# The odd layer's input projection with seven block products per set in place of eight

## The chip, the cores and the metric

The kernel runs on one core of a Trainium2 chip. The metric is the device time of one execution in microseconds, the median of several. Times inside an execution come from one profiled execution and are counted from the start of its span.

## The reference, cut to what matters

The model has two layers over 1024 latent tokens of width 1024; all numbers are fp32. The second (odd) layer mixes tokens with a gated short convolution:

```python
def short_conv_mixer(h, w_in, conv_w, conv_b, w_out):
    gb, gc, u = jnp.split(h @ w_in, 3, axis=-1)          # w_in: 1024 x 3072
    up = jnp.pad(gc * u, ((0, 0), (1, 1), (0, 0)))
    y = up[:, :-2] * conv_w[0] + up[:, 1:-1] * conv_w[1] + up[:, 2:] * conv_w[2] + conv_b
    return (gb * y) @ w_out
```

`h @ w_in` is the product that the change touches. A layer norm comes before it (the end of the even layer), the product with `w_out` and a mixture of experts behind it.

## The kernel before, in words

Each engine has its own program, and the programs meet at semaphores. The queue of SyncE (SP) issues nearly all loads. The stages around the change run in this order.

**End of the even layer.** For each of eight tiles of 128 tokens, TensorE (PE) sums the experts' rows and the residual (L1215, L1230), VectorE (DVE) and ScalarE (ACT) normalize the tile (L1759 to L1774, L1409, L1411), and one tile later PE transposes it (`stream_T`, L673). ACT and DVE evict four of the eight 128x128 blocks each into `u1T` (L1283, L1527), which holds the normed stream with channels on partitions: 8 slices of 128 input channels by 1024 tokens. `tile_a` and `tile_d` count the evictions. Around the last transposes PE runs dummy matmuls (`fill`, L680). The weights of the first two output chunks come in six loads of 512 KB between the tiles' loads.

**Input projection.** `conv_chunk` takes one chunk of 128 channels out of 1024, and for it the three parts m = 0 (gb), 1 (gc) and 2 (u). For each half of the tokens (512) it makes three sums over 8 slices of input channels, in three banks. ACT copies gc and gb out of PSUM (L1501, L1502), DVE multiplies u by gc into `conv_in` (L2094), and after both halves it applies the three taps and the gate over 1024 tokens (L2101 to L2107) into `zT`. Eight chunks, four turns of a loop of two. At the start of this stage DVE also applies the last scale and shift of the even layer's norm to all eight tiles (`affine`, L2049 and L2051). GpSimd (POOL) has nothing to do here.

**Output projection.** `odd_first` does tile 0: seven of eight slices of both halves, and the eighth when the last chunk's `zT` is there. It needs `w_out` in two loads of 2 MB, the first released by the first half of the last chunk, the second by its end. Tiles 1 to 7 follow with their transposes and router logits, then the experts.

## Time and profile before

| what | value |
|---|---|
| runs shown | 2442.22, 2440.99 and 2446.84 us, median 2442.22 |
| profiled execution: its span | 2442.1 us |
| profiled execution: its own time | no separate figure; the median of the runs is 0.1 us above the span |
| TensorE matmuls busy | 2338.8 us, 96% of the span |
| VectorE / ScalarE / GpSimd busy | 765.4 / 421.8 / 280.3 us |
| input projection of the odd layer | 1369.7 to 1699.4 us, matmuls busy 329.8 us |
| granted TensorE clock in that stretch | 1.00 |

"Busy" is the time in which the profile shows an instruction on the engine. An fp32 matmul of 512 columns shows as two instructions of 592 ns that overlap, 0.43 us apart, so that one matmul takes 0.859 us of the engine.

### The profile page before, as it was taken

To read this page: it belongs to the slowest core of one execution; us is meant where nothing else is said; L and a number is where in the kernel's file an instruction comes from. 1 tells how busy PE (TensorE), PEld (TensorE's weight loads), DVE (VectorE), ACT (ScalarE), POOL (GpSimd) and SP (SyncE) were. 2 spreads that over 40 slices of the span, in tenths; PEclk is the share of its full clock that TensorE was granted. 3 is DMA by queue.
4 is the path that set the end of the run, shared out by engine and by line. 5 is a ranking of instruction groups with operands and counts; after the bars stand their busy time and mean duration, and the time that the engine had idled before them with its cause. 6 is when DMAs were issued, how large, how long until landed. Compare 5 with 4: busy or idle time off the path is not lost.

```text
span 2442.1 us, 28217 instructions
## 1 busy us (share of the span) xinstructions
PE 2338.8 (96%) x10546; PEld 1167.6 (48%) x10546; DVE 765.4 (31%) x1697; ACT 421.8 (17%) x920; POOL 280.3 (11%) x341
## 2 busy tenths in 40 slices
PE   6989999999999999999999999999998999999997
PEld 3546547888555344443334444444554444443332
DVE  3694114555537111111113511111345111111115
ACT  2301133444221111101012200000111111101111
POOL 0000103323222200000000000000232100000000
PEclk8999999999999999999999999999998999999999
DMA  9881000000316999999898210102208999999987
GB/s 386 307 347 58 0 1 1 2 18 20 124 52 231 418 419 413 410 414 409 356 419 311 94 52 26 52 26 75 106 31 320 409 418 407 418 406 419 391 352 258
DMA packets 147602, 572.34 MB, mean 234 GB/s; under 512 B 25065, under 2 KB 50825, under 8 KB 104970
## 3 DMA queue, kind: packets, MB, share of 16 engines
q1 hardware_dynamic: 134218, 536.97, 55.6%
q0 software_dynamic: 13248, 33.57, 3.6%
q8 instruction: 84, 1.38, 0.2%
q14 instruction: 52, 0.43, 0.0%
HBM read 549.51 MB, written 35.65 MB: 240 GB/s over the span
## 4 chain that ended last, share of the span: by engine, by line
PE 83%; DMA 5%; DVE 5%; SPq 2%; issue 2%; ACT 1%; POOL 1%; DVEq 0%; POOLq 0%; ACTq 0%
PE bank L1116 23%; PE bank L1199 14%; PE bank L1140 12%; PE bank L722 8%; PE bank L1032 5%; PE bank L992 4%; PE bank L825 3%; PE bank L673 3%; DVE lnwb L1569 2%; DMA bigA<-in_moe_w 2%; SPq L450 2%; PE bank L1230 2%; PE bank L839 1%; PE bank L808 1%; PE bank L1215 1%
## 5 line engine op out<-in xcount | busy, mean ns | idle before, releaser
L1116 PE MATMUL bank<-bigA,bigB 128*32 128x512 f32 (+2 forms) x1888 | 427.7, 598 | 7.5 <-ACT bigB L1283 7.5
L1199 PE MATMUL bank<-bigB,bigA 128*128 128x512 f32 x768 | 329.8, 592 | 1.2 <-ACT bigB L1283 1.2
L722 PE MATMUL bank<-bigC,bigB 128*128 128x512 f32 (+3 forms) x768 | 292.0, 536 | 0.0
L1116 PE MATMUL bank<-bigC,bigB 128*128 128x512 f32 (+2 forms) x800 | 283.4, 594 | 0.0
L1140 PE MATMUL bank<-bigA,bigB 128*32 128x512 f32 (+2 forms) x1120 | 272.1, 604 | 9.8 <-DMA bigA<-in_moe_w 8.7
L1116 PEld LDWEIGHTS bank<-bigA,bigB 128*32 128x32 f32 (+2 forms) x1888 | 146.4, 134 | 226.2 <-issue 214.9
L1199 PEld LDWEIGHTS bank<-bigB,bigA 128*128 128x128 f32 x768 | 145.8, 190 | 185.2 <-issue 185.2
L722 PEld LDWEIGHTS bank<-bigC,bigB 128*128 128x128 f32 x768 | 142.1, 192 | 127.5 <-issue 119.4
L1283 ACT ACTIVATE bigB<-bank,small 128x128 f32<-128x128 f32 x296 | 110.3, 461 | 364.7 <-PE bank L673 364.6
L1116 PEld LDWEIGHTS bank<-bigC,bigB 128*128 128x128 f32 (+2 forms) x800 | 101.6, 153 | 142.4 <-issue 142.1
L1140 PEld LDWEIGHTS bank<-bigA,bigB 128*32 128x32 f32 (+2 forms) x1120 | 96.1, 139 | 147.7 <-issue 144.3
L2213 POOL DMA_INDIRECT y_rows<-bigB,ints x44 | 44.4, 1008 | 845.8 <-DVE bigB L1996 845.8
L1996 DVE TENSOR_TENSOR bigB<-bank,gate 128x512 f32<-128x512 f32 x88 | 56.7, 686 | 250.3 <-PE bank L1140 250.3
L1987 DVE TENSOR_TENSOR bigB<-bigB,bank 128x512 f32<-128x512 f32 x44 | 30.3, 688 | 295.4 <-PE bank L1116 295.4
L1424 ACT ACTIVATE bigB<-bank 128x512 f32<-128x512 f32 x44 | 26.3, 597 | 534.3 <-PE bank L1116 534.3
L992 PE MATMUL bank<-bigB,bigA 128*128 128x512 f32 x256 | 112.9, 594 | 2.0 <-DMA bigB<-in_w_out_odd 2.0
L2197 POOL TENSOR_TENSOR bigC<-bigC,lnwb 128x1024 f32<-128x1024 f32 x16 | 37.7, 2354 | 609.2 <-PE bank L673 609.2
L1991 DVE COPY bigB<-bank 128x256 f32<-128x256 f32 x44 | 18.7, 424 | 255.3 <-PE bank L1124 255.3
L2094 DVE TENSOR_TENSOR bigA<-bank,bigA 128x512 f32<-128x512 f32 x16 | 11.1, 692 | 263.6 <-ACT bigA L1502 263.6
L1569 DVE SCALAR_TENSOR_TENSOR lnwb<-bigA,normw,lnwb 128x1024 f32<-128x1024 f32 x70 | 89.9, 1284 | 9.6 <-DMA bigA<-in_ada_w 5.4
L825 PE MATMUL bank<-bigB 128*128 128x128 f32 x608 | 83.8, 284 | 7.6 <-issue 6.6
L825 PEld LDWEIGHTS bank<-bigB 128*128 128x128 f32 x608 | 72.7, 191 | 17.5 <-issue 15.0
(295 smaller groups left out, 2329.5 us busy)
## 6 DMA issues: line engine op xcount, KB each, us to landing
bigA<-in_moe_w SPq DMA_DIRECT2D x292, 1024.0 KB, 19.2
bigC<-in_moe_w SPq DMA_DIRECT2D x92, 1024.0 KB, 19.4
bigA<-in_ada_w SPq DMA_DIRECT2D x40, 1024.0 KB, 7.1
bigA<-y_rows SPq DMA_DIRECT2D x14, 1024.0 KB, 5.5
bigA<-in_w_in_odd SPq DMA_DIRECT2D x24, 512.0 KB, 6.1
bigA<-in_ada_w SPq DMA_DIRECT2D x4, 2048.0 KB, 12.5
...
```

The costliest lines, as they stand in the source:

```text
L450: sp.dma_start(dst, src, **how).then_inc(S(name), 16)
L673: last = tp(bank(b + k // 4)[:, (k % 4) * P:(k % 4 + 1) * P], cols(src, n)[:, k, :], ident)
L722: last = mm(bank(n % 3)[:, 0:w], uT[:, k, t * P:(t + 1) * P], wring[:, g % 2, k, at_:at_ + w], start=(k == 0), stop=(k == KC - 1))
L825: last = mm(dst, sc[:, p % 3, g, k * P:(k + 1) * P], unit_p[:, p % 2, g, :], start=True, stop=True, skip_group_check=True)
L992: last = mm(bank(2 * (t % 2) + n), zT[:, k, t * P:(t + 1) * P], wout1[:, k, n * 512:(n + 1) * 512], start=(k == 0), stop=(k == KC - 1))
L1032: last = mm(bank(2 * (t % 2) + n), lhs[:, k, :], wout[k0 + k][:, n * 512:(n + 1) * 512], start=(k0 + k == 0), stop=(k0 + k == KC - 1), ski ...
L1116: last = mm(bank(m)[at_:at_ + w, :], xT[:, j, KC // 2 * h + k, at_:at_ + w], w13_at(SLOT_OF[m, h, q][0], k), start=(h == 0 and k == 0), st ...
L1140: last = mm(bank(6 + n)[at_:at_ + w, :], gT[:, 2 * h + k, at_:at_ + w], w2_at(SLOT_OF[2, h, q][0], k)[:, n * 512:(n + 1) * 512], start=(h ...
L1199: last = mm(bank(3 * half + m), wc[:, j, m, k, :], u1T[:, k, half * 512:(half + 1) * 512], start=(k == 0), stop=(k == KC - 1))
L1283: last = go(dst[k], bank(b + k // 4)[:, (k % 4) * P:(k % 4 + 1) * P], ACT.Identity, bias=shift[:, k:k + 1], scale=scale[:, k:k + 1])
L1569: V(v.scalar_tensor_tensor(acc[:, r % 2], part, cond[:, k, 0:1], acc[:, r % 2], MUL, ADD))
L1996: v.tensor_tensor(yo[:, j, n * 512:(n + 1) * 512], bank(6 + n), gate[:, 1, n * 512:(n + 1) * 512], MUL)\
```

## The change

The projection is cut into twelve sets: four pairs of channel chunks, each for m = 1, 2, 0. A set is a product of 256 output channels by 1024 input channels by 1024 tokens, seen as 2x2 blocks: A11, A12, A21, A22 of the weights (128 output channels by 512 input channels) and B11, B12, B21, B22 of the stream (512 input channels by 512 tokens). The eight block products are replaced by seven, of sums and differences of the blocks (Winograd's form of Strassen's scheme); each is four matmuls of 128x512. PE makes them in the order 1, 2, 6, 5, 7, 3, 4:

- 1 = A11 B11 and 2 = A12 B21, on loaded data (`conv_first`); 1 + 2 is the first output block;
- 6, 5, 7, 3, 4 (`conv_rest`) use sums: 6 is added to 1 in its bank, 7 to that, 4 to that; 5 has a bank of its own, to which 3 is added.

ACT copies a bank's state out of PSUM between products (after 1, 6, 5 and, but for m = 2, 4), and DVE adds copies and banks to make the output blocks. The sums of weight blocks (four operations of 128x512 a set) are made by POOL. The sums of stream blocks are made once: by POOL for token tiles 4, 5 and 6 (`token_sums`, three operations of 512 elements and two of 256 a tile), by DVE for tile 7. The scale and shift of `affine` is spread over the sets of m = 1 and 2. The loop becomes straight code. `conv_first` of set 0 and of set 1 take the places of the two groups of dummy matmuls around the last transposes. Weights come as one load of 1 MB a set, two of them between the tiles' loads. The banks of the output projection's tiles are swapped.

```diff
-        wc = at(bigA, 12288, 2, 3, KC, P)
-        conv_in = at(bigA, 18432, 2, SEQ + 2)
-        conv_b2, conv_u, conv_y = at(bigA, 0, 2, SEQ), at(bigA, 2048, 2, 512), at(bigA, 3072, SEQ)
+        wc = [at(bigA, 12288 + 2560 * j, KC, 2 * P) for j in range(2)]
+        wc_s1 = [at(bigA, 12288 + 2560 * j + 2048, 4, P) for j in range(2)]
+        conv_in = at(bigA, 0, 2, SEQ + 2)
+        part1, part2, part5 = normw[:, :], [at(bigA, 2304 + 512 * j, 512) for j in range(2)], at(bigA, 3328, 512)
+        conv_y = cst[:, C_AT["cos"][0]:C_AT["cos"][0] + SEQ]
+
+        SETS = [(cp, m) for cp in range(KC // 2) for m in (1, 2, 0)]
+        SUM_BANK, SIDE_BANK, CROSS_BANK = (4, 0), (5, 1), (2, 3)
+        u_sum2, u_sum3 = at(bigA, 17408, 4, 512), at(bigA, 19456, 4, 512)
+        u_sum4 = [at(bigA, 23552, 2, 512), lowT[:, 0:8, :].rearrange("p (k h) i -> p k (h i)", k=2)]
...
+        conv_order = [(s, n) for s in range(2) for n in (1, 2)]
+        for _s in range(len(SETS)):
+            conv_order += [(_s, n) for n in ((1, 2) if _s >= 2 else ()) + (6, 5, 7, 3, 4)]
+        copy_order = [(s, n) for s, (_, m) in enumerate(SETS) for n in ((1, 2, 5) if m == 2 else (1, 2, 5, 4))]
+        sum_order = [(s, n) for s, (_, m) in enumerate(SETS) for n in ((11, 22, 12, 21) if m == 2 else (11, 22, 12))]
...
+        def c21_done(s):
+            return summed(s, 21) if SETS[s][1] == 2 else copied(s, 4)
+
+        def conv_dst(s, row, half):
+
+            cp, m = SETS[s]
+            if m == 0:
+                return zT[:, 2 * cp + row, 512 * half:512 * half + 512]
+            return conv_in[:, row, 1 + 512 * half:513 + 512 * half]
...
-                w_odd = T["w_in_odd"][0].rearrange("(p k) (m c n) -> p m k c n", k=KC, m=3, n=P)
+                w_odd = T["w_in_odd"][0].rearrange("(p k) (m c n) -> p m k c n", k=KC, m=3, n=2 * P)
...
+                def conv_weights(s):
+                    cp, m = SETS[s]
+                    load(wc[s % 2], w_odd[:, m, :, cp, :], f"wc_in{s % 2}")
...
-                    if l == 0 and 1 <= t < NT - 1:
-                        c, m = (t - 1) // 3, (t - 1) % 3
-                        load(wc[:, c, m], w_odd[:, m, :, c, :], f"wc_in{c}")
+                    if l == 0 and t in (1, 3):
+                        conv_weights(t // 2)
...
+                for s in range(2, len(SETS)):
+                    sp.wait_ge(*made(s - 2, 4))
+                    conv_weights(s)
                 sp.wait_ge(S("ln"), 2 * NT)
                 ln_params(1, 0)
                 router(1)
-                with sp.Fori(0, NT // 2 - 1) as i:
-                    for j in range(2):
-                        c = 2 * i + j
-                        sp.wait_ge(S("conv_mm"), 2 * c + 2)
-                        for m in range(3):
-                            load(wc[:, j, m], w_odd[:, m, :, bass.ds(c + 2, 1), :].squeeze(2), f"wc_in{j}")
                 w_o = T["w_out_odd"][0].rearrange("(k p) n -> p k n", p=P)
-                sp.wait_ge(S("conv_mm"), 15)
+                sp.wait_ge(*made(len(SETS) - 1, 2))
                 load(wout1[:, :, 0:512], w_o[:, :, 0:512], "wout_in")
-                sp.wait_ge(S("conv_mm"), 16)
+                sp.wait_ge(*made(len(SETS) - 1, 3))
                 load(wout1[:, :, 512:], w_o[:, :, 512:], "wout_g")
-                sp.wait_ge(S("z_ok"), KC + 2)
+                sp.wait_ge(S("z_ok"), KC)
                 for n in range(EARLY[1]):
                     piece(1, n)
...
-                pe.wait_ge(S("conv_a"), 2 * KC + 1)
-                pe.wait_ge(S("z_ok"), KC + 1)
+                pe.wait_ge(*summed(len(SETS) - 1, 12))
+                pe.wait_ge(S("z_ok"), KC - 2)
                 pe.wait_ge(S("wout_in"), 80)
-                odd_part(0, 0, 0, KC - 1)
+                odd_part(0, 0, 0, KC - 2)
                 pe.wait_ge(S("wout_g"), 32)
-                odd_part(0, 1, 0, KC - 1)
-                pe.wait_ge(S("z_ok"), KC + 2)
+                odd_part(0, 1, 0, KC - 2)
+                pe.wait_ge(*copied(len(SETS) - 1, 4))
+                pe.wait_ge(S("z_ok"), KC)
                 for n in range(2):
-                    odd_part(0, n, KC - 1, KC).then_inc(S("out_mm"), 1)
+                    odd_part(0, n, KC - 2, KC).then_inc(S("out_mm"), 1)
...
-            def conv_chunk(i, j):
-
-                c = 2 * i + j
-                pe.wait_ge(S(f"wc_in{j}"), 48 * (i + 1))
-                for half in range(2):
-
-                    pe.wait_ge(S("conv_a"), 2 * c + half + 1)
-                    pe.wait_ge(S("conv_d"), 2 * c + half + 1)
-                    for m in range(3):
-                        for k in range(KC):
-                            last = mm(bank(3 * half + m), wc[:, j, m, k, :], u1T[:, k, half * 512:(half + 1) * 512],
-                                      start=(k == 0), stop=(k == KC - 1))
-                    last.then_inc(S("conv_mm"), 1)
+            def product(s, b, lhs, rhs, first):
+
+                for k in range(4):
+                    last = mm(bank(b[s % 2]), lhs[:, k, :], rhs(k), start=(first and k == 0), stop=(k == 3),
+                              skip_group_check=True)
+                last.then_inc(S("conv_mm"), 1)
+
+            def quarter(s, row, half):
+
+                return wc[s % 2][:, 4 * half:4 * half + 4, row * P:(row + 1) * P]
+
+            def conv_first(s):
+
+                pe.wait_ge(S(f"wc_in{s % 2}"), 16 * (s // 2 + 1))
+                if s >= 2:
+                    pe.wait_ge(*c21_done(s - 2))
+                product(s, SUM_BANK, quarter(s, 0, 0), lambda k: u1T[:, k, 0:512], True)
+                if s >= 2:
+                    pe.wait_ge(*summed(s - 2, 11))
+                product(s, SIDE_BANK, quarter(s, 0, 1), lambda k: u1T[:, 4 + k, 0:512], True)
+
+            def conv_rest(s):
+
+                pe.wait_ge(S("u_sums"), 4)
+                pe.wait_ge(*copied(s, 1))
+                pe.wait_ge(S("w_sum"), 3 * s + 2)
+                product(s, SUM_BANK, quarter(s, 0, 0), lambda k: u_sum2[:, k, :], False)
+                if s >= 2:
+                    pe.wait_ge(*summed(s - 2, 12))
+                product(s, CROSS_BANK, wc_s1[s % 2], lambda k: u1T[:, k, 512:], True)
+                pe.wait_ge(*copied(s, 2))
+                product(s, SUM_BANK, quarter(s, 1, 0), lambda k: u_sum3[:, k, :], False)
+                pe.wait_ge(*copied(s, 5))
+                pe.wait_ge(S("w_sum"), 3 * s + 3)
+                product(s, CROSS_BANK, quarter(s, 0, 1), lambda k: u1T[:, 4 + k, 512:], False)
+                pe.wait_ge(*summed(s, 22))
+                product(s, SUM_BANK, quarter(s, 1, 1), lambda k: u_sum4[k // 2][:, k % 2, :], False)
...
-            fill(4, 2)
+            pe.wait_ge(S("tile_a"), NT + 4)
+            pe.wait_ge(S("tile_d"), NT + 4)
+            conv_first(0)
             stream_T(NT - 1)
-            fill(4, 1)
-            pe.wait_ge(S("tile_a"), 2 * NT)
-            pe.wait_ge(S("tile_d"), 2 * NT)
-            with pe.Fori(0, KC // 2) as i:
-                for j in range(2):
-                    conv_chunk(i, j)
+            conv_first(1)
+            for s in range(len(SETS)):
+                if s >= 2:
+                    conv_first(s)
+                conv_rest(s)
...
-            act.sem_inc(S("conv_a"), 2)
-            with act.Fori(0, KC // 2) as i:
-                for j in range(2):
-                    c = 2 * i + j
-                    for half in range(2):
-                        act.wait_ge(S("conv_mm"), 2 * c + half + 1)
-                        if half == 0:
-                            act.wait_ge(S("z_ok"), c + 1)
-                        go(conv_u[:, half], bank(3 * half + 1), ACT.Copy)
-                        go(conv_b2[:, j, half * 512:(half + 1) * 512], bank(3 * half), ACT.Copy).then_inc(S("conv_a"), 1)
+            def conv_copies(s):
+
+                cp, m = SETS[s]
+                act.wait_ge(*made(s, 1))
+                if s:
+                    act.wait_ge(*summed(s - 1, 11))
+                go(part1, bank(SUM_BANK[s % 2]), ACT.Copy).then_inc(S("conv_a"), 1)
+                act.wait_ge(*made(s, 6))
+                if s >= 2:
+                    act.wait_ge(*summed(s - 2, 12))
+                go(part2[s % 2], bank(SUM_BANK[s % 2]), ACT.Copy).then_inc(S("conv_a"), 1)
+                act.wait_ge(*made(s, 5))
+                if s:
+                    act.wait_ge(*summed(s - 1, 22))
+                go(part5, bank(CROSS_BANK[s % 2]), ACT.Copy).then_inc(S("conv_a"), 1)
+                if m != 2:
+                    act.wait_ge(*made(s, 4))
+                    if m == 1 and cp:
+                        act.wait_ge(S("z_ok"), 2 * cp)
+                    go(conv_dst(s, 1, 0), bank(SUM_BANK[s % 2]), ACT.Copy).then_inc(S("conv_a"), 1)
...
+            dve.wait_ge(S("tile_a"), 2 * NT)
+            dve.wait_ge(S("tile_d"), 2 * NT)
+            tok7 = slice(3 * P, 4 * P)
+            far7 = slice(7 * P, 8 * P)
+            V(v.tensor_tensor(u_sum3[:, :, tok7], u1T[:, 4:, far7], u1T[:, 0:4, far7], SUB))
+            V.wait()
+            V(v.tensor_tensor(u1T[:, 0:4, far7], u1T[:, 0:4, far7], u1T[:, 0:4, tok7], SUB))
+            V.wait()
+            V(v.tensor_tensor(u_sum2[:, :, tok7], u1T[:, 4:, far7], u1T[:, 0:4, far7], SUB))
+            V.wait()
+            for h in range(2):
+                V(v.tensor_tensor(u_sum4[h][:, :, tok7], u1T[:, 4 + 2 * h:6 + 2 * h, tok7], u_sum2[:, 2 * h:2 * h + 2, tok7], SUB))
+            V.wait()
+            v.sem_inc(S("u_sums"), 1)
...
-            v.sem_inc(S("conv_d"), 2)
-            v.sem_inc(S("z_ok"), 2)
-            for t in range(NT):
-                affine(0, t)
...
+                v.scalar_tensor_tensor(zT[:, c, :], conv_y, convp[:, 3, c:c + 1], zT[:, c, :], ADD, MUL).then_inc(S("z_ok"), 1)
+
+            def gathered_sum(s, row, half, part, b):
+
+                dst = conv_dst(s, row, half)
+                if SETS[s][1] != 2:
+                    v.tensor_tensor(dst, part, bank(b[s % 2]), ADD).then_inc(S("conv_d"), 1)
+                    return
+                V(v.tensor_tensor(part, part, bank(b[s % 2]), ADD))
+                V.wait()
+                v.tensor_tensor(dst, dst, part, MUL).then_inc(S("conv_d"), 1)
...
+            def conv_set(s):
+
+                cp, m = SETS[s]
+                if m == 1 and cp:
+                    gated_taps(cp - 1)
+                dve.wait_ge(*made(s, 2))
+                dve.wait_ge(*copied(s, 1))
+                if m == 2:
+                    dve.wait_ge(*summed(s - 1, 12))
+                    dve.wait_ge(*c21_done(s - 1))
+                gathered_sum(s, 0, 0, part1, SIDE_BANK)
+                if m == 0:
+                    dve.wait_ge(*summed(s - 1, 12))
+                    dve.wait_ge(*c21_done(s - 1))
+                    for n in range(3):
+                        tap(2 * cp, n)
+                else:
+                    affine(0, 2 * cp + m - 1)
+                dve.wait_ge(*made(s, 7))
+                dve.wait_ge(*copied(s, 5))
+                gathered_sum(s, 1, 1, part5, SUM_BANK)
+                dve.wait_ge(*made(s, 3))
+                dve.wait_ge(*copied(s, 2))
+                gathered_sum(s, 0, 1, part2[s % 2], CROSS_BANK)
+                if m == 2:
+                    dve.wait_ge(*made(s, 4))
+                    dst = conv_dst(s, 1, 0)
+                    v.tensor_tensor(dst, dst, bank(SUM_BANK[s % 2]), MUL).then_inc(S("conv_d"), 1)
+
+            def gated_taps(cp):
+
+                s = 3 * cp + 2
+                dve.wait_ge(*summed(s, 12))
+                z_rows(2 * cp)
+                dve.wait_ge(S("z_ok"), 2 * cp + 1)
+                for n in range(3):
+                    tap(2 * cp + 1, n)
+                dve.wait_ge(*c21_done(s))
+                z_rows(2 * cp + 1)
+                dve.wait_ge(S("z_ok"), 2 * cp + 2)
+
+            for s in range(len(SETS)):
+                conv_set(s)
+            gated_taps(KC // 2 - 1)
...
+            def weight_sums(s):
+
+                w = wc[s % 2]
+                pool.wait_ge(S(f"wc_in{s % 2}"), 16 * (s // 2 + 1))
+                G(pool.tensor_tensor(wc_s1[s % 2], w[:, 0:4, P:], w[:, 4:, P:], ADD))
+                G.wait()
+                pool.tensor_tensor(w[:, 0:4, P:], w[:, 0:4, 0:P], w[:, 0:4, P:], SUB).then_inc(S("w_sum"), 1)
+
+            def weight_sums_late(s):
+
+                w = wc[s % 2]
+                pool.wait_ge(S("w_sum"), 3 * s + 1)
+                pool.wait_ge(*made(s, 1))
+                pool.tensor_tensor(w[:, 0:4, 0:P], wc_s1[s % 2], w[:, 0:4, 0:P], SUB).then_inc(S("w_sum"), 1)
+                pool.wait_ge(S("w_sum"), 3 * s + 2)
+                pool.wait_ge(*made(s, 2))
+                pool.tensor_tensor(w[:, 4:, 0:P], w[:, 4:, 0:P], w[:, 0:4, 0:P], SUB).then_inc(S("w_sum"), 1)
+
+            def token_sums(t):
+
+                near, far = slice((t - 4) * P, (t - 3) * P), slice(t * P, (t + 1) * P)
+                pool.wait_ge(S("tile_a"), NT + t + 1)
+                pool.wait_ge(S("tile_d"), NT + t + 1)
+                G(pool.tensor_tensor(u_sum3[:, :, near], u1T[:, 4:, far], u1T[:, 0:4, far], SUB))
+                G.wait()
+                G(pool.tensor_tensor(u1T[:, 0:4, far], u1T[:, 0:4, far], u1T[:, 0:4, near], SUB))
+                G.wait()
+                G(pool.tensor_tensor(u_sum2[:, :, near], u1T[:, 4:, far], u1T[:, 0:4, far], SUB))
+                G.wait()
+                for h in range(2):
+                    G(pool.tensor_tensor(u_sum4[h][:, :, near], u1T[:, 4 + 2 * h:6 + 2 * h, near],
+                                         u_sum2[:, 2 * h:2 * h + 2, near], SUB))
+                G.wait()
+                pool.sem_inc(S("u_sums"), 1)
+
+            weight_sums(0)
+            for t in range(4, NT - 1):
+                token_sums(t)
+            weight_sums_late(0)
+            for s in range(1, len(SETS)):
+                weight_sums(s)
+                weight_sums_late(s)
```

## Rows read from the trace of the kernel before

**Rows 1.** The page's head: span, and busy time of each engine.
```profile
span 2442.1 us, 28217 instructions
PE 2338.8 (96%) x10546; PEld 1167.6 (48%) x10546; DVE 765.4 (31%) x1697; ACT 421.8 (17%) x920; POOL 280.3 (11%) x341
```
**Rows 2.** The page's chain that ended last, by line.
```profile
PE bank L1116 23%; PE bank L1199 14%; PE bank L1140 12%; PE bank L722 8%; PE bank L1032 5%; PE bank L992 4%; PE bank L825 3%; PE bank L673 3%; DVE lnwb L1569 2%; DMA bigA<-in_moe_w 2%; SPq L450 2%; PE bank L1230 2%; PE bank L839 1%; PE bank L808 1%; PE bank L1215 1%
```
**Rows 3.** Line L1199's own view: ns min/median/max, and who waited.
```profile
L1199 PE MATMUL bank<-bigB,bigA x768: 592/592/667, 1369.7 to 1699.0; 128*128 128x512 f32 x192
...
  ACT bigA L1501: 314.1, 16
```
**Rows 4.** The chain in order of time: start us, us, what.
```profile
863.27 7.06 PE bank L1116 x16
870.80 6.87 PE bank L1116 x16
...
1306.04 3.96 issue
1310.00 5.39 PE bank L1215 x8
1320.94 5.78 DMA bigA<-h_rows
1369.71 329.85 PE bank L1199 x768
1699.58 7.94 DMA bigB<-in_w_out_odd
```
**Rows 5.** PE's timeline ahead of the projection: start us, us, instructions [idle before].
```profile
1363.57 1.88 PE L680 MATMUL bank<-cst 128*128 128x512 f32 x4
1366.51 1.16 PE L673 MATMUL bank<-cst,bigC 128*128 128x128 f32 x8 [1.06 <-ACT bigC L1411]
...
1369.71 22.55 PE L1199 MATMUL bank<-bigB,bigA 128*128 128x512 f32 x52 [1.18 <-ACT bigB L1283]
```
**Rows 6.** ACT's timeline: evictions of tiles 5, 6 and 7, then the first copy.
```profile
1360.33 1.50 ACT L1283 ACTIVATE bigB<-bank,small 128x128 f32<-128x128 f32 x4
...
1366.36 2.90 ACT L1283 ACTIVATE bigB<-bank,small 128x128 f32<-128x128 f32 x8
1390.67 0.60 ACT L1501 ACTIVATE bigA<-bank 128x512 f32<-128x512 f32 x1 [21.41 <-PE bank L1199]
```
**Rows 7.** POOL's groups over the whole span, shapes apart: busy, mean ns | idle.
```profile
L2197 POOL TENSOR_TENSOR bigC<-bigC,lnwb 128x1024 f32<-128x1024 f32 x16 | 37.7, 2354 | 609.2 <-PE bank L673 609.2
...
L2135 POOL TENSOR_TENSOR bigA<-bigA,normw 128x512 f32<-128x512 f32 x8 | 9.9, 1272 | 292.2 <-ACT bigA L1329 292.2
```
**Rows 8.** DVE L1851 and L1786, POOL L2199: ns min/median/max of each.
```profile
L1851 DVE TENSOR_TENSOR bigB<-bigB x14: 191/192/2228, 767.1 to 1848.3; 128x32 f32<-128x32 f32 x14
...
L1786 DVE SCALAR_TENSOR_TENSOR bigA<-bigC,bigA x16: 691/692/1024, 1715.5 to 1832.5; 128x512 f32<-128x512 f32 x16
...
L2199 POOL TENSOR_TENSOR bigC<-bigC,lnwb x16: 2347/2391/2676, 650.6 to 1840.0; 128x1024 f32<-128x1024 f32 x16
```
**Rows 9.** ACT's and DVE's groups between 1363 and 1710 us.
```profile
L1501 ACT ACTIVATE bigA<-bank 128x512 f32<-128x512 f32 x16 | 9.6, 597 | 314.1 <-PE bank L1199 314.1
...
L2094 DVE TENSOR_TENSOR bigA<-bank,bigA 128x512 f32<-128x512 f32 x16 | 11.1, 692 | 263.6 <-ACT bigA L1502 263.6
L2105 DVE SCALAR_TENSOR_TENSOR bigA<-bigA,small 128x1024 f32<-128x1024 f32 x8 | 10.3, 1285 | 1.9 <-DVE bigA L2103 1.4
...
L2051 DVE TENSOR_TENSOR bigC<-bigC,lnwb 128x1024 f32<-128x1024 f32 x8 | 9.8, 1225 | 0.3
```
**Rows 10.** PE's timeline at the output projection, and where the second experts begin.
```profile
1707.56 14.86 PE L992 MATMUL bank<-bigB,bigA 128*128 128x512 f32 x34 [2.00 <-DMA bigB<-in_w_out_odd]
...
1868.95 8.78 PE L1116 MATMUL bank<-bigA,bigB 128*64 128x512 f32 x32 [2.14 <-ACT bigB L1283]
```
**Rows 11.** Windows: us, busy of PE, PEld, DVE, ACT, POOL, PEclk, DMA share, GB/s.
```profile
1850.00:2226.00 376.00, 369.40 (x1587) 159.15 (x1589) 74.55 (x181) 42.62 (x104) 41.87 (x48) 0.98 0.99 404
```

44 lines of the change are left out of this document (22 added, 22 removed).

## The prediction

> **What bounds the kernel now.** I read the head of the page first, then the chain that ended last, the conv line's own view, and the timelines around it. The head [rows 1] shows a span of 2442.1 us with TensorE's matmuls busy for 2338.8 of them; no other engine is busy for a third of it. The chain [rows 2] says the same in another way: the largest pieces are all matmul lines, and L1199, the product that the change rewrites, is 14% of it. One busy engine proves little, so the second question is whether that line is held up by anything. It is not. Its 768 instructions are one unbroken piece of 329.85 us [rows 4], through 16 semaphore waits and 8 chunks, and the only large wait tied to it goes the other way: ScalarE waits 314.1 us for it [rows 3], the idle time of its first copy in each half being the product's length. An instruction is 329.85/768 = 0.4295 us, a matmul 0.859 us. So a matmul taken out here is time taken out, as long as the smaller steps that replace it stay hidden.
>
> The result is compared with the median of the runs, 2442.2 us. It is 0.1 us above the span; I carry that 0.1 along unchanged.
>
> **Removed: an eighth of the matmuls.** Before: 8 chunks x 2 halves x 3 parts x 8 slices = 384. After: 12 sets x 7 products x 4 = 336. 48 fewer of 0.859 us are **-41.2 us**. The shape stays 128x128 by 128x512, so the price per matmul should too.
>
> **Moved: two sets' first products over the wait for the last tile.** Before, the engine makes dummies from 1363.57, waits 1.06 us, transposes, makes one more dummy and waits 1.18 us, until 1369.71 [rows 5]: 6.14 us, of which only the transposes (some 0.9 us) are needed. After, products 1 and 2 of set 0 (8 x 0.859 = 6.87 us) start at 1363.57, the transposes follow at 1370.4, products 1 and 2 of set 1 at 1371.3, to 1378.2. All these matmuls are counted in the 336. The gain is 6.14 - 0.9 = **-5.2 us**. The price is that the last tile is transposed 3.9 us later (1370.4, not 1366.5), so what hangs on it is late; that comes next.
>
> **Added: sums of stream blocks, needed at 1378.2.** Product 6 of set 0 needs all four tiles' sums and a weight sum. GpSimd first. No row shows 512 elements beside other work, but 128x1024 takes 2.35 us and 128x512 1.27 us [rows 7]; on that line 256 elements are about 0.73 us. A tile is 3 x 1.27 + 2 x 0.73 = 5.3 us, some 5.5 with gaps. Tile 5 is evicted at 1361.8, tile 6 at half of ScalarE's eight evictions, 1367.8 [rows 6]; the cadence of 6 us is longer than 5.5, so nothing piles up and GpSimd ends tile 6 at about 1373.3. Its next operation, the weight sum that product 6 needs, ends by 1375 if nobody is in its way. If GpSimd were half as fast again, it would end three tiles at 1380 and miss by 3 us; I take the rows.
>
> VectorE's tile 7: the pair transposes-to-ready took 1366.51 to 1369.71, 3.2 us, with ScalarE still busy on the tile before [rows 5, 6]; without that it is about 2.8, so the tile is ready at 1373.3. Its five sums go in four dependent steps. Nearest rows: 0.69 us for 128x512, 0.19 for 128x32 [rows 8, 9], so about 0.42 for 256 elements; 3 x 0.69 + 2 x 0.42 plus four gaps of 0.1 = 3.3 us. Alone they end at 1376.6 and are hidden by 1.6 us.
>
> They are not alone. The rows that worried me most are those of shared operations [rows 8]. A VectorE sum of 128x32 that takes 0.19 us took 2.23 us once, and a 128x512 one went from 0.69 to 1.02; GpSimd's own 1024-element line goes from 2.35 to 2.68. In the one case VectorE lost a whole operation of GpSimd, in the other a third of a microsecond. From 1373.3 on GpSimd has six operations of 1.27 us queued without a pause (two late weight sums of set 0, four of set 1), so both readings can be priced. Reading one, 0.33 us per step: 1376.6 + 4 x 0.33 = 1377.9, no stall. Reading two, a whole operation of GpSimd between each two of VectorE's steps: 3 x 1.27 = 3.8 us more, 1380.4, a stall of 2.2; with one more ahead of the first step 1381.7, a stall of 3.5. The 2.23 us row is the cleaner one, since the 1.02 us could be the rest of an operation almost over, so I take **+2.5 us** for this wait, and keep 0 and 6.
>
> The Trainium skill (SBUF — State Buffer, Who interferes with whom) states that a VectorE instruction with two SBUF inputs and a GpSimd instruction that reads SBUF exclude each other for the whole instruction, whichever is first. By that rule the sum is the one with +2.5; by the 0.33 us row taken as the whole price it would be 2.5 us less.
>
> **Added: ScalarE's copies between products.** A copy is 0.60 us [rows 9]; the first one before started 0.3 us after its matmuls (1369.71 + 48 x 0.4295 = 1390.33, start 1390.67) [rows 5, 6]. In each set a product of 3.44 us lies between the product whose bank is copied and the next that adds to it (1, copy, then 2, then 6; 6, copy, 5, then 7; 5, copy, 7, then 3), so 0.3 + 0.6 + about 0.3 to restart hides behind 3.44. There is one exception. Set 1 has its first products already made, so its product 6 comes directly behind product 4 of set 0, and ScalarE, in order, first copies set 0's last bank and then set 1's first. Before product 6 lie 0.3 + 0.60 + 0.50 + up to 0.45 of restart (from the end of the last eviction, 1369.26, to 1369.71 [rows 5, 6]) = 1.4 to 1.85 us: **+1.7 us**, once. Sets 2 to 11 have products 1 and 2 in that place, 6.87 us.
>
> **Added: VectorE and GpSimd in the steady state.** A set takes 28 x 0.859 = 24.1 us. VectorE's heaviest set (m = 1) holds a gate, three taps, a gate (5 x 1.28 = 6.4 at most), three sums of 0.69 and an affine of 2 x 1.22: 10.9 us, hidden [rows 9]. GpSimd: 4 x 1.27 = 5.1, hidden. What could bite is the order. Product 6 needs the weight sum that starts after product 1; it has product 2 (3.44 us) for 0.3 + 1.27, and if one tap or gate of VectorE holds it up by 1.28 still 0.6 us is left. Product 4 needs VectorE's sum 22, released by product 7 and covered by product 3: 0.3 + 0.69 against 3.44. Affine and taps lie behind sum 11, with 10.3 us to product 7's end; at double length they fit. I cost all of it at 0. With a cover gone, each set would pay a wait of 1 us or so.
>
> **Added: 84 product ends instead of 16.** The nearest row is an experts' group of two times four matmuls with a wait in the middle: 6.87 us, the price of eight matmuls and nothing more; another is 7.06 [rows 4]. I take 0; 0.19 for every two products would be 8 us. Straight code in place of the loop: 0, the experts' lines run that way.
>
> **Moved: weight loads.** Set 0's 1 MB replaces 0.5 MB ahead of tile 2's loads, and tile 2's residual is on the chain for 5.78 us [rows 4]. 2 MB of `w_out` land in 7.94 us, so half a megabyte more is 2.0 us at most; some of it has drained by then, and later tiles carry less. **+0.3 us**, between 0 and 2. The other ten loads come a whole set ahead. The output projection's second load of 2 MB is released one product earlier, 3.44 us before the end, and lands 7.94 us after: 4.5 us after the end. Six matmuls (5.15 us) now stand before it, so the 2.00 us wait [rows 10] goes: **-2.0 us**. The last channels: sum 12, gate, three taps, gate are 0.69 + 5 x 1.28 and gaps, 7.6 us at most from the end of product 3; product 4 and twelve matmuls are 13.7. Hidden. The experts behind it are partly bound by their weights (DMA share 0.99 [rows 11]), but those loads are released by the same events as before and shift as a whole.
>
> **Sum.** -41.2 - 5.2 + 2.5 + 1.7 + 0.3 - 2.0 = -43.9. 2442.2 - 43.9 = **2398.3 us**.
>
> **The rivals.** *The clock drops in the new waits.* After a wait of 3.96 us, eight instructions took 5.39 us instead of 3.44 [rows 4]; after one of 2.14 us, 32 took 8.78 instead of 6.87 (two share the array) [rows 10]; after 2.00 us, 34 took 14.86, almost nothing more. Each of my two new waits may cost 1.9 more, and the first may be 3.5 to 6: 2400 to 2406. Chance 0.22. *The block sums are hidden after all* (reading one): 2395.8. For it speaks the 1.02 us row. Chance 0.15. *Every hand-over costs*, up to 8 us, or the denser work of the other engines brings the clock to the 0.98 of the experts' stretch [rows 11], 289 x 0.02 = 6 us: 2402 to 2406. Against it: nothing of this in the unbroken 329.85. Chance 0.08. *Slower:* the weight sum that product 6 waits for is late in every set, because VectorE's two-input operations keep GpSimd out. With S us of wait in each of twelve sets the gain is gone at S = 43.9/12 = 3.7, and slower by 0.3% at 4.3, that is 2450 at 4.3. GpSimd would have to be held up by 1.9 us of slack plus 3.7, four gates or taps in a row, where at most two of them fall in one set of three. Chance 0.02; a partial gain within 0.3% of before 0.02.
>
> **How the numbers follow.** The forecast itself has 0.51. 0.3% of 2442 is 7.3 us, about what runs of this kernel can tell from nothing (they lie 5.9 us apart). All cases but the last two are faster by more: 0.96. Its own range is 2396 to 2401. The whole range takes in the hidden sums, a median of runs a microsecond or two lower, the larger first wait with a clock drop, and hand-over costs: 2392 to 2406.
>
> **What the profile after would show.** 672 instructions in the product line, 0.4295 us apart, busy 288.6 us. A first wait of 2 to 3.5 us before product 6 of set 0, put down to VectorE's block sums, whose five operations show lengths of up to 2 us. A second of 1.4 to 1.9 us some 17 us later, behind a ScalarE copy, and no third. No wait for `w_out`. Output projection and experts as long as before. The prediction is wrong if product 6 waits in every set, if the granted clock falls below 1.00 in the stretch, or if the tile cadence before it changes by more than a microsecond.

## The result, and the profile after

| | before | after |
|---|---|---|
| median of 4 runs each, taken in turn | 2442.89 us (2440.99 to 2446.84) | 2399.84 us (2397.52 to 2402.47) |
| ratio, 95% interval | | 0.982 (0.9809 to 0.9832) |
| span of the profiled execution | 2442.1 us | 2395.7 us |

The forecast was 2398.3 us; the time lies 1.5 us above it, inside the 2396 to 2401 given for the likeliest case. The medians differ by 43.1 us, the two spans by 46.4. The change unedited was measured twice more beside the kernel before (e1_again and e10_again below), with medians 44.3 and 46.3 us apart.

The head of the page after, to be laid beside [rows 1], and its chain by line, beside [rows 2]; the product is L1226 now:

```profile
span 2395.7 us, 28049 instructions
...
PE 2292.7 (96%) x10444; PEld 1145.4 (48%) x10444; DVE 818.5 (34%) x1738; ACT 430.1 (18%) x932; POOL 371.4 (16%) x404
...
PE bank L1150 24%; PE bank L1174 12%; PE bank L1226 12%; PE bank L755 8%; PE bank L1066 5%; PE bank L1025 5%; PE bank L706 3%; PE bank L858 3%; DVE lnwb L1642 2%; DMA bigA<-in_moe_w 2%; SPq L482 2%; PE bank L1288 2%; PE bank L872 1%; PE bank L841 1%; DMA bigA<-h_rows 1%
```

TensorE is busy 46.1 us less. It still bounds the kernel: the sums have cost other engines time, not taken its place.

The product line's own view (PE rows: ns min/median/max, first and last start), to be laid beside [rows 3]:

```profile
L1226 PE MATMUL bank<-bigB,bigA x384: 592/592/595, 1365.9 to 1655.2; 128*128 128x512 f32 x192
...
L1226 PE MATMUL bank<-bigA x240: 592/592/697, 1382.8 to 1656.9; 128*128 128x512 f32 x120
...
L1226 PE MATMUL bank<-lowT,bigA x48: 592/592/593, 1398.4 to 1658.6; 128*128 128x512 f32 x48
```

384 + 240 + 48 = 672 instructions. Where two followed each other at once they were 0.4295 us apart, as before: 16 in 6.87 us. And TensorE's timeline at the start of the product, beside [rows 5]:

```profile
1365.90 7.03 PE L1226 MATMUL bank<-bigB,bigA 128*128 128x512 f32 x16
1372.77 1.04 PE L706 MATMUL bank<-cst,bigC 128*128 128x128 f32 x8
1373.65 7.03 PE L1226 MATMUL bank<-bigB,bigA 128*128 128x512 f32 x16
1382.82 3.70 PE L1226 MATMUL bank<-bigA 128*128 128x512 f32 x8 [2.14 <-DVEq L2166]
...
1398.38 1.88 PE L1226 MATMUL bank<-lowT,bigA 128*128 128x512 f32 x4
1401.48 3.67 PE L1226 MATMUL bank<-bigA 128*128 128x512 f32 x8 [1.22 <-issue]
```

Products 1 and 2 of set 0, the transposes of the last tile, products 1 and 2 of set 1. Then the first wait, 2.14 us, before product 6 of set 0; then, after product 4 (the row with `lowT`), the second, 1.22 us, before product 6 of set 1. There is no third until 1659.06, and the chain in order of time has the rest of the product as one piece:

```profile
1401.48 257.74 PE bank L1226 x600
```

That "issue" in the last row of the timeline stands as the releaser means only that the profile found no event to name; ScalarE's rows further down do.

At the other end of the product, beside [rows 10]:

```profile
1659.06 20.76 PE L1025 MATMUL bank<-bigB,bigA 128*128 128x512 f32 x48
...
1822.81 8.78 PE L1150 MATMUL bank<-bigA,bigB 128*64 128x512 f32 x32 [2.12 <-ACT bigB L1342]
```

48 instructions of the output projection in one piece: the 2.00 us wait for `w_out` is gone, the second experts begin behind the same wait as before.

**The span by stages** (us; the bounds are starts of rows of TensorE's timeline). A: from the last group of 32 experts' instructions of the even layer (1302.42 before, 1303.33 after) to the first product or the dummies it displaced. B: to the output projection's first row. C: to the four dummies at the second router. D: to the ten dummies behind it. E: to the end. The later rows are those of the experiments below.

| profile | A | B | C | D | E |
|---|---|---|---|---|---|
| before | 61.2 | 335.8 | 134.5 | 24.2 | 584.0 |
| after | 62.6 | 293.2 | 132.2 | 21.4 | 583.0 |
| e1_again | 63.3 | 293.2 | 132.2 | 23.5 | 582.3 |
| e10_again | 64.6 | 294.9 | 132.2 | 21.7 | 584.1 |
| e2_pool_waits | 63.0 | 291.2 | 132.2 | 23.7 | 585.3 |
| e3_copy_first | 63.4 | 291.7 | 132.2 | 22.8 | 586.3 |
| e4_eighth | 62.4 | 336.0 | 132.2 | 23.6 | 581.7 |
| e5_fills | 61.7 | 295.7 | 132.9 | 22.8 | 584.5 |
| e6_wout_late | 62.5 | 293.2 | 135.3 | 21.5 | 585.7 |
| e7_loads | 60.7 | 292.6 | 132.2 | 23.4 | 583.0 |
| e9_best | 62.1 | 289.5 | 132.2 | 22.9 | 588.3 |

B is 42.7 us shorter and C 2.3. The rest of the span's 46.4 is D, 2.8 less, and 1.0 in E, against 1.4 more in A and 0.9 more before it. B and C are steady: the three profiles of the unedited change agree on them within 0.1 us, but for one step of 1.7 us in B (e10_again, below). A, D and E differ by 2 us each between these three, and over the whole table D by 2.8 and E by 6.6 us, where no edit bears on them. So a term of the sum is read in its own stage, not in the total.

### The profile page after: what moved, and what is told of

The parts are those of the page before. It is cut to its first block, busy times and chain, and to the rows that moved or that the text cites. A ratio compares the mean times of both kernels' runs of the same rounds, so it can differ in the third digit from the quotient of the medians.

```text
span 2395.7 us, 28049 instructions
## 1 busy us (share of the span) xinstructions
PE 2292.7 (96%) x10444; PEld 1145.4 (48%) x10444; DVE 818.5 (34%) x1738; ACT 430.1 (18%) x932; POOL 371.4 (16%) x404
## 4 chain that ended last, share of the span: by engine, by line
PE 83%; DMA 6%; DVE 5%; SPq 2%; issue 2%; ACT 1%; POOL 1%; DVEq 0%; POOLq 0%; ACTq 0%
PE bank L1150 24%; PE bank L1174 12%; PE bank L1226 12%; PE bank L755 8%; PE bank L1066 5%; PE bank L1025 5%; PE bank L706 3%; PE bank L858 3%; DVE lnwb L1642 2%; DMA bigA<-in_moe_w 2%; SPq L482 2%; PE bank L1288 2%; PE bank L872 1%; PE bank L841 1%; DMA bigA<-h_rows 1%
## 5 line engine op out<-in xcount | busy, mean ns | idle before, releaser
L2346 POOL DMA_INDIRECT y_rows<-bigB,ints x44 | 44.3, 1007 | 845.4 <-DVE bigB L2069 845.4
L1226 PE MATMUL bank<-bigB,bigA 128*128 128x512 f32 x384 | 170.7, 592 | 0.0
L1226 PEld LDWEIGHTS bank<-bigB,bigA 128*128 128x128 f32 x384 | 72.8, 190 | 90.9 <-issue 90.9
L1025 PE MATMUL bank<-bigB,bigA 128*128 128x512 f32 x256 | 112.7, 594 | 0.0
L1226 PE MATMUL bank<-bigA 128*128 128x512 f32 x240 | 109.0, 593 | 3.4 <-DVEq L2166 2.1
L1600 DVE TENSOR_SCALAR bigB<-bank,small 128x128 f32<-128x128 f32 x216 | 73.8, 404 | 25.3 <-PE bank L706 22.2
```

What stands on the lines that cost most here:

```text
L1025: last = mm(bank(2 * ((t + 1) % 2) + n), zT[:, k, t * P:(t + 1) * P], wout1[:, k, n * 512:(n + 1) * 512], start=(k == 0), stop=(k == KC - 1))
L1226: last = mm(bank(b[s % 2]), lhs[:, k, :], rhs(k), start=(first and k == 0), stop=(k == 3), skip_group_check=True)
L1600: last = v.tensor_scalar(dst[k], bank(b + 1)[:, (k - 4) * P:(k - 3) * P], scale[:, k:k + 1], shift[:, k:k + 1], MUL, ADD)
```

## The experiments

Each ran beside the kernel before on the same chip, in three groups: e1_again to e4_eighth (kernel before: 2444.17 us), e5_fills to e8_half (2445.02 us), e9_best and e10_again (2444.93 us). Line numbers of edited kernels are off by one to three where a line was added ahead.

**The same kernel again (e1_again, e10_again).** No edit.

> The changed kernel once more, without an edit, as the base of the next runs. Expected: 2397 to 2402 us and a ratio to before of 0.982. In the trace the first wait of the projection (before product 6 of set 0) 2.1 us, the second (before product 6 of set 1) 1.2 us, no third. One question is open: the stretch of the second router took 24.2 us before and 21.4 in the profile of the changed kernel. Theory A: this is where a drop of the granted clock falls, and varies from run to run. Theory B: it is a steady effect of the change, and comes again at 21.4.

> The changed kernel with no edit once more, beside the version with the three edits. Theory: 2400 us (2398 to 2402), ratio 0.982, with 2.1 us of wait before product 6 of set 0, 1.2 us before product 6 of set 1, and a stretch after the second router anywhere from 21.4 to 24.2 us. If this stretch comes out at 21.4 again, it goes with the change more often than with the kernel before; if at 23 or more, the shorter one in the first profile of the changed kernel was this execution's own.

Measured: 2399.88 us, ratio 0.982 (0.9803 to 0.9836), and 2398.64 us, 0.9812 (0.9798 to 0.9825). First waits of 2.15 and 2.16 us, second 1.22 in both, none for `w_out`. D came out at 23.5 and 21.7, so the shorter stretch at the router is neither in every profile of the change nor in one alone: the three shortest, 21.4 to 21.7, are the ones where the twelve dummies in it ran slowly. The rows of after:

```profile
1798.27 7.09 PE L713 MATMUL bank<-cst 128*128 128x512 f32 x12
...
1812.68 6.25 PE L713 MATMUL bank<-cst 128*128 128x512 f32 x10
```

And the same rows of e1_again:

```profile
1798.86 5.40 PE L713 MATMUL bank<-cst 128*128 128x512 f32 x12
...
1815.28 6.16 PE L713 MATMUL bank<-cst 128*128 128x512 f32 x10
```

The slower row, 7.09 us, stands in the shorter stretch. In after, e6_wout_late and e10_again the low clock falls on the dummies, which nobody waits for, and the router's small steps behind them run at full clock; in the other eight of the table it falls on those steps. After, the granted clock was 0.79 from 1798 to 1806, where the dummies stand, and 0.98 from 1806 to 1813; in e1_again it was 1.00 from 1799 to 1805 and 0.66 from 1805 to 1815. The mean granted clock of the stretch was 0.92 after (1791 to 1813) and 0.82 before (1834 to 1858). In what the profiles show, the place of the drop goes with no edit, though all three short ones are of the new arithmetic; with one profile of the kernel before among the eleven, that stays open.

**Which wait is the first one: GpSimd starts its weight sums behind VectorE's block sums (e2_pool_waits).** It makes set 0's two late sums as before, then waits.

```diff
             weight_sums_late(0)
+            pool.wait_ge(S("u_sums"), 4)
             for s in range(1, len(SETS)):
```

> GpSimd waits for all block sums of the stream before it starts the weight sums of set 1 (only the two late weight sums of set 0 are still beside VectorE's sums). Theory 1 (VectorE's sums are long because each gives way to a whole GpSimd operation): VectorE's five sums go from 7.3 us to 4.5 to 6, and the first wait from 2.1 us to between 0 and 0.8; total 1.5 to 2 us less. Rival (VectorE's sums are slow by their own access patterns, or a third of a microsecond is lost to each anyway): sums stay near 7 us, wait near 2, total unchanged.

VectorE's five sums for the last token tile, in the unedited kernel after:

```profile
1375.39 1.18 DVE L2157 TENSOR_TENSOR bigA<-bigB 128x512 f32<-128x512 f32 x1 [0.17 <-ACT bigB L1342]
1376.60 1.63 DVE L2159 TENSOR_TENSOR bigB<-bigB 128x512 f32<-128x512 f32 x1
1378.27 1.64 DVE L2161 TENSOR_TENSOR bigA<-bigB 128x512 f32<-128x512 f32 x1
1379.94 1.37 DVE L2164 TENSOR_TENSOR bigA<-bigB,bigA 128x256 f32<-128x256 f32 x1
1381.24 1.48 DVE L2164 TENSOR_TENSOR lowT<-bigB,bigA 128x256 f32<-128x256 f32 x1
```

GpSimd beside them:

```profile
1375.29 0.73 POOL L2422 TENSOR_TENSOR lowT<-bigB,bigA 128x256 f32<-128x256 f32 x1
1376.27 1.42 POOL L2405 TENSOR_TENSOR bigA<-bigA 128x512 f32<-128x512 f32 x1 [0.25 <-POOL lowT L2422]
1377.76 1.59 POOL L2408 TENSOR_TENSOR bigA<-bigA 128x512 f32<-128x512 f32 x1
1379.33 1.71 POOL L2396 TENSOR_TENSOR bigA<-bigA 128x512 f32<-128x512 f32 x1
```

The same five in e2_pool_waits:

```profile
1375.13 1.19 DVE L2157 TENSOR_TENSOR bigA<-bigB 128x512 f32<-128x512 f32 x1 [0.17 <-ACT bigB L1342]
1376.35 1.64 DVE L2159 TENSOR_TENSOR bigB<-bigB 128x512 f32<-128x512 f32 x1
1378.02 1.64 DVE L2161 TENSOR_TENSOR bigA<-bigB 128x512 f32<-128x512 f32 x1
1379.69 0.42 DVE L2164 TENSOR_TENSOR bigA<-bigB,bigA 128x256 f32<-128x256 f32 x1
1380.03 0.42 DVE L2164 TENSOR_TENSOR lowT<-bigB,bigA 128x256 f32<-128x256 f32 x1
```

Each length is the operation plus the time in which GpSimd's held it up: the starts of the two engines' rows alternate, 1376.27, 1376.60, 1377.76, 1378.27, 1379.33, 1379.94. With GpSimd standing still, the last two fall from 1.37 and 1.48 to 0.42 us; the 512-element ones, still beside it, keep 1.64 instead of 0.69. Start to end the five took 7.3 us, with the edit 5.3; alone they would be 3.3 as estimated. The wait went: product 6 starts 7.17 us after set 1's first product (1373.39, 1380.56), with no idle time noted. B fell by 2.0. The time, 2399.22 us, ratio 0.9809 (0.9791 to 0.9826), does not show it apart from the unedited change.

**Which wait is the second one: ScalarE copies set 1's first bank early (e3_copy_first).** In `conv_copies(0)`, between the copy of product 5 and the wait for product 4:

```diff
+                if s == 0:
+                    first_copy(1)
                 if m != 2:
                     act.wait_ge(*made(s, 4))
```

(`first_copy` is the first copy of a set, taken out of `conv_copies`, which leaves it out for set 1; the semaphore's order of copies is changed to match.)

> ScalarE copies the first bank of set 1 before it waits for product 4 of set 0. Theory 1 (product 6 of set 1 waits for ScalarE's order alone): the second wait goes from 1.2 us to 0 and the total falls by 1.2. Rival (the wait is for GpSimd's weight sum or for the hand-over after product 4): it stays at 1.2.

In the unedited kernel after, ScalarE's timeline between product 4's end and product 6's start at 1401.48 is:

```profile
1400.30 0.60 ACT L1572 ACTIVATE bigA<-bank 128x512 f32<-128x512 f32 x1 [9.70 <-PE bank L1226]
1400.79 0.59 ACT L1559 ACTIVATE normw<-bank 128x512 f32<-128x512 f32 x1
```

Product 4's copy first (`L1572`), set 1's (`L1559`) behind it, and TensorE 0.10 us after that. With the order changed, TensorE's timeline has no wait there:

```profile
1398.68 1.88 PE L1227 MATMUL bank<-lowT,bigA 128*128 128x512 f32 x4
1400.40 3.60 PE L1227 MATMUL bank<-bigA 128*128 128x512 f32 x8
```

B fell by 1.5. The time was 2402.85 us, ratio 0.9829 (0.9814 to 0.9844): the mechanism is shown, the gain of 1.2 us is not seen in the total. The median lies 3.0 us above e1_again's, with intervals that overlap; A and E of its profile were 0.9 and 3.2 us longer than after's.

**The eighth product put back (e4_eighth).** Four more matmuls a set, ahead of product 4, into a bank that nobody reads; everything else stays.

```diff
+                for k in range(4):
+                    mm(bank(6), quarter(s, 1, 1)[:, k, :], u_sum4[k // 2][:, k % 2, :], start=(k == 0), stop=(k == 3), ...)
                 pe.wait_ge(*summed(s, 22))
```

> An eighth product of four matmuls is made in each set, into a bank that nobody reads, before product 4; everything else stays. Theory 1 (the gain is the matmul count, all else hidden): 12 x 4 x 0.859 = 41.2 us more, near 2441, so the whole change without the count saves about 2 us. Rival (part of what VectorE, ScalarE and GpSimd do shows in each set and would be covered by the additional product): less than 38 us more.

Measured: 2440.34 us, ratio 0.9986 (0.9973 to 0.9999), 40.5 us above the change beside it; B 336.0, 42.9 above. 41.2 of those are the matmuls. The other 1.7 stand in one row, the first product behind the first wait:

```profile
1383.23 5.34 PE L1226 MATMUL bank<-bigA 128*128 128x512 f32 x8 [2.18 <-DVEq L2169]
```

5.34 us where after has 3.70. The extra matmuls come later, so they are not the cause, and e10_again has the same with no edit (5.40 us behind 2.16; the granted clock there was 1.00 in the 16 us to 1383 and 0.73 in the 4 us from 1387, a mean of the levels of 1.2 and 2.4 GHz). It is the clock rival of the prediction. Of the six profiles of whole products with this wait at 2.1 us or more, two have the drop: after, e1_again, e3_copy_first and e6_wout_late have 3.70. e8_half, below, has it too, behind a longer wait.

**The products moved back behind the dummies (e5_fills).** `fill(4, 2)` and `fill(4, 1)` stand again where they stood, and `conv_first(0)` and `conv_first(1)` behind the last tile.

```diff
-            conv_first(0)
+            fill(4, 2)
             stream_T(NT - 1)
+            fill(4, 1)
...
+            conv_first(0)
             conv_first(1)
```

> The first products of sets 0 and 1 are moved back behind the last tile's transposes and evictions, and the dummy matmuls stand in front again. Theory 1: the 5.2 us of dummies and waits come back, and the first wait (2.1 us) goes, since 13.7 us of products now follow the tile's evictions: 3 us more in all. Rival (the move was worth nothing, or the first wait has nothing to do with it): 0, or 5 us more with the wait still there.

Measured: 2401.81 us, ratio 0.9813 (0.98 to 0.9826). The dummies begin at 1364.74, the products at 1370.48, 5.74 us later; 6.14 was the figure before. Beside them there was no first wait. From 1364.74 and 1366.46 (e1_again) to the output projection are 295.7 and 293.2 us: the move is worth 2.5, its 4.9 us (5.74 less 0.88 of transposes) less the wait of 2.15 that it brings (2.30 from the last product to the next).

C was 0.7 us longer than after's, with a wait for `w_out` that no other profile with the load released by product 3 of a whole set has:

```profile
1666.15 15.72 PE L1025 MATMUL bank<-bigB,bigA 128*128 128x512 f32 x36 [0.40 <-DMA bigB<-in_w_out_odd]
```

So the six matmuls cover that load with little to spare.

**The second load of `w_out` one product later (e6_wout_late).** Released by product 4 in place of 3.

```diff
-                sp.wait_ge(*made(len(SETS) - 1, 3))
+                sp.wait_ge(*made(len(SETS) - 1, 4))
```

> The second load of the output weights is released by product 4 of the last set instead of product 3. Theory 1: it lands 7.9 us after the end of the projection, where six matmuls cover 5.2, so 2.8 us of wait for it come back. Rival (the wait of before went for another reason): no wait.

```profile
1668.51 15.72 PE L1025 MATMUL bank<-bigB,bigA 128*128 128x512 f32 x36 [2.88 <-DMA bigB<-in_w_out_odd]
```

The wait is back at 2.88 us, C 3.2 longer; 2406.55 us, ratio 0.9835 (0.9817 to 0.9854). That is 6.8 us above e7_loads beside it, twice what the wait explains; the four runs spread over 10 us, and the rest stays open. In C, what keeps the old 2.00 us away is that the load is released one product before the end.

**The weight loads later among the tiles (e7_loads).** With tiles 3 and 5 in place of 1 and 3.

```diff
-                    if l == 0 and t in (1, 3):
-                        conv_weights(t // 2)
+                    if l == 0 and t in (3, 5):
+                        conv_weights(t // 2 - 1)
```

> The weight loads of sets 0 and 1 are issued with the tiles 3 and 5 of the end of the even layer instead of 1 and 3. Theory 1 (1 MB ahead of tile 2's loads holds these up): the waits for y_rows (0.6 us) and h_rows (1.35 us) of tiles 1 and 2 become shorter, together by 1 to 2 us, and the tile cadence of 6.0 us stays. Rival (the waits come from the tiles' own loads, or tile 5 is now held up): the end of the even layer is as long as in the changed kernel, some 66.0 us from its last experts' product to the first product of set 0.

TensorE's waits for data at the start of the tiles in the kernel after, two rows of its timeline. The first stands before the second half of tile 0's product with `y_rows` (the expectation puts it at tile 1), whose load is issued ahead of the weights'; the second before tile 2's residual, whose load is issued behind them.

```profile
1320.24 1.98 PE L1288 MATMUL bank<-bigA,bigB 128*128 128x512 f32 x4 [0.64 <-DMA bigA<-y_rows]
...
1329.61 1.98 PE L1273 MATMUL bank<-bigA,alpha_i 128*128 128x512 f32 x4 [1.35 <-DMA bigA<-h_rows]
```

In e7_loads the first was gone and the second 0.15 us:

```profile
1327.71 1.98 PE L1273 MATMUL bank<-bigA,alpha_i 128*128 128x512 f32 x4 [0.15 <-DMA bigA<-h_rows]
```

Nine profiles have the loads at tiles 1 and 3 (e8_half is one). In all nine tile 2's residual is waited for by 1.03 to 1.49 us, against 0.19 before, 0.15 here and nothing in e9_best, below; tile 0's second half by 0.20 to 1.26 in seven of the nine and in none of the other three. A was 60.7 us, where the nine have 61.7 to 64.6, 63.1 in the mean, and before 61.2. e9_best has 62.1 with the later loads, so 61.4 is the mean of the two. The loads as the change places them cost TensorE about 1.7 us, with a spread as large as that. The time was 2399.79 us, ratio 0.9807 (0.9794 to 0.9821).

The first wait of the products was 1.63 us here, not 2.1: VectorE's second sum took 1.10 us beside one of GpSimd's operations of 256 elements, where it takes 1.63 beside one of 512. The size of this wait depends on where the two streams meet.

**How much room the sums have (e8_half).** Only slices 0 and 3 of each product's four are made: half of the contraction is left out, a set has 12.0 us of matmuls instead of 24.1, and VectorE, ScalarE and GpSimd do all that they did.

```diff
-                for k in range(4):
+                for k in (0, 3):
```

> Only the first and the last of each product's four matmuls are made, so half of the contraction is left out: 168 matmuls instead of 336, all copies, sums and loads as they were. It asks how far VectorE, ScalarE and GpSimd are from being the bound. Theory 1 (they are far from it): 144 us of matmuls go and only the start pays, since the first products cover half as long, so some 2255 to 2265 us and fewer than 1 us of waits in a set. Rival (their order and the shared port bind soon): 1 to 4 us of waits in every set of 12 us, 2270 to 2300 us.

One execution, 2275.35 us. The first wait was 5.31 us, now for GpSimd, which had less product time to work behind. In the steady state a set took 12.9 us (from 1401.47 to 1504.89 are eight), 0.9 over its matmuls, and waits of 0.26 to 1.11 us, 4.3 in all, stood before the last product of six of the eight, as in this row:

```profile
1425.92 1.12 PE L1226 MATMUL bank<-bigA 128*128 128x512 f32 x2 [1.11 <-DVE bigA L2191]
```

It is for VectorE's sum, not for a weight sum of GpSimd. The 0.9 us a set is what the first theory expected. The total is in the rival's range: 19.8 us above the 2399.84 less the 144.3 of the matmuls left out. But only about half of that comes from waits in the sets. The first wait is 3.2 us longer, and C 4.5 us longer with a 2.50 us wait for `w_out`, which a shorter product 4 no longer covers. Behind both the instructions ran slowly:

```profile
1380.05 3.75 PE L1226 MATMUL bank<-bigA 128*128 128x512 f32 x4 [5.31 <-POOL bigA L2405]
...
1537.26 17.41 PE L1025 MATMUL bank<-bigB,bigA 128*128 128x512 f32 x36 [2.50 <-DMA bigB<-in_w_out_odd]
```

Four instructions behind the second wait, of 1.22 us, took 1.96, and the same 36 took 15.72 behind 2.88 us in e6_wout_late: 1.8 and 1.7 us more.

**The three edits that took a wait away, together (e9_best).** Those of e2_pool_waits, e3_copy_first and e7_loads.

> Three edits of the changed kernel together: GpSimd starts its weight sums after VectorE's first block sums, ScalarE copies set 1's first bank before it waits for product 4 of set 0, and the two weight loads go with token tiles 3 and 5 in place of 1 and 3. Theory: each takes away the wait that it took away alone, so the profile shows no wait of over 0.3 us before product 6 of set 0 (2.1 before) nor before product 6 of set 1 (1.2 before), and the stage from the last experts' burst to the first product at 60.5 to 61.5 us (62.6 to 63.3 before). Sum: 2.1 + 1.2 + 1.5 = 4.8 us less, so a median near 2395.5 and a ratio to the kernel before of 0.980 (0.979 to 0.982). Rival: the time saved in these stages does not reach the end, because the stretch after the second router (21.4 to 24.2 us in the profiles so far) and the other stages move by as much from run to run: waits gone in the profile, a median within 1 us of the unedited kernel's that runs beside it.

Measured: 2395.58 us, ratio 0.98 (0.9786 to 0.9815), against 2398.64 (e10_again) beside it. Neither wait is left:

```profile
1375.28 7.03 PE L1227 MATMUL bank<-bigB,bigA 128*128 128x512 f32 x16
1382.30 3.70 PE L1227 MATMUL bank<-bigA 128*128 128x512 f32 x8
...
1397.86 1.88 PE L1227 MATMUL bank<-lowT,bigA 128*128 128x512 f32 x4
1399.57 3.60 PE L1227 MATMUL bank<-bigA 128*128 128x512 f32 x8
```

B is 289.5 us, 3.6 less than after: 288.6 for the 672 instructions, 0.9 for the transposes, and nothing between them. The medians differ by 3.1 us of the 4.8 expected, but the two intervals overlap: the best version run, not shown to be faster than the change. In its one profile the gain did not arrive, the span being 2400.5 as e10_again's 2400.6. E was 588.3 instead of 584.1, and there is 2.2 us more ahead of A. In this profile the later loads also moved a part of their price to tile 6 (in e7_loads they did not), whose residual is issued just behind the load placed with tile 5:

```profile
1355.36 1.98 PE L1274 MATMUL bank<-bigA,alpha_i 128*128 128x512 f32 x4 [1.40 <-DMA bigA<-h_rows]
```

## Why the prediction was right

- **The matmuls, -41.2.** Right: 672 instructions of 0.4295 us. e4_eighth gives the same 41.2 back in B, beside the 1.7 of its slow row.
- **First products over the last tile's wait, -5.2.** Right in B: from 1365.90 the products run through, and only the 0.88 us of transposes lie between. Undone alone (e5_fills) it was 4.9.
- **First wait, +2.5.** Right, and for the reason taken: e2_pool_waits stops GpSimd and the wait is gone. From the end of set 1's first products, 1373.65 + 6.87 = 1380.52, to product 6 it is 2.30 us, of which the row notes 2.14 as idle. The stage began 2.3 us later than in the forecast, and with that taken off the steps fall where they were put: GpSimd's last tile sum at 1373.7 (1373.3 forecast), VectorE's tile ready at 1372.9 (1373.3), its last sum done at 1380.4 (1380.4). Reading two was the right one; that the 1.02 us row of before [rows 8] was the rest of an operation almost over stays an argument. The Trainium skill (SBUF — State Buffer, Who interferes with whom) has the rule, and this trace agrees, in both directions: VectorE's 0.69 us became 1.63, GpSimd's 1.27 became 1.42 to 1.71.
- **Second wait, +1.7.** From product 4's end, 1398.38 + 4 x 0.4295 = 1400.10, to 1401.48: 1.38 us, 1.22 of it noted as idle, behind the two copies, as e3_copy_first shows. The restart was 0.10 us, not up to 0.45, which gives the lower end of the forecast; the wait that the row notes lies below it.
- **Steady state, 0.** Right, and with room: after the first two waits there is none in the rest of the twelve sets. The operations did collide, as the groups of 1365.9 to 1656 show:

```profile
L2180 DVE SCALAR_TENSOR_TENSOR cst<-bigA,small,cst 128x1024 f32<-128x1024 f32 x14 | 23.3, 1665 | 0.5
L2398 POOL TENSOR_TENSOR bigA<-bigA 128x512 f32<-128x512 f32 x11 | 21.8, 1977 | 0.9
...
L2124 DVE TENSOR_TENSOR bigC<-bigC,lnwb 128x1024 f32<-128x1024 f32 x8 | 16.4, 2054 | 0.3
```

  Taps of 1665 ns in the mean where [rows 9] has 1285, weight sums of 1977 where GpSimd's 512 elements take 1272 [rows 7], affine of 2054 where it was 1225. All of it lies beside products. With sets half as long 0.9 us a set comes through, and for VectorE's sum, so the slower rival, a weight sum late by 3.7 us in every set, has nothing for it.
- **Product ends, 0.** Right: B after, 293.16, is 288.6 + 0.88 + 2.30 + 1.38, with nothing left for 80 hand-overs. The granted clock was 1.00 in the stretch.
- **Weight loads, +0.3.** Mis-sized. A is 1.4 us longer, and e7_loads puts 1 to 2 us on the loads. The bound of 2.0 held in the mean (A is 1.9 us longer than before over the nine profiles, 3.4 in the longest); the value was too low. The step that failed is "some of it has drained by then, and later tiles carry less": tile 2's residual came 1.03 to 1.49 us late in every profile with these loads, against 0.19 before. The sum also left out tile 0's second half, issued ahead of the weights, which came 0.64 us late after and up to 1.26 in other profiles. The steady cadence of the tiles stayed (6.0 us), but the step from tile 1 to tile 2 went from 6.50 to 7.65 us, 1.15 more, just over the microsecond that the prediction named as a sign of being wrong.
- **`w_out`, -2.0.** Right: C is 2.3 less, and e6_wout_late brings back 2.88. The cover is thin, as the 0.40 us in e5_fills shows.
- **Output projection and experts as long as before.** Right for the output projection. For the rest it was a claim that one profile can't carry: D and E move by up to 2.8 and 6.6 us between profiles. In this pair they came out 3.8 us shorter. The profiled execution of the change is also the fastest of its four, 2397.52 us, 2.3 below the median, and so the spans' 46.4 exceeds the medians' 43.1.
- **The clock rival (0.22)** was real as a mechanism and small: 1.7 us in two of the six profiles with a first wait of 2.1 to 2.2 us. The second wait, 1.22 us, never brought it. It belonged into the forecast as a third of its price, 0.6 us, rather than as a case apart.

In B and C the sum gave -44.2 and the profile has -44.9; in A it gave +0.3 and the profile has +1.4. That these two misses nearly cancel is luck. So is an agreement of the total within 1.5 us: three measurements of the same gain gave 43.1, 44.3 and 46.3 us, where the forecast had 43.9.
